# First three projection units multiplied with the unnormed x, with their sums scaled afterwards

## The chip, the cores and the metric

The kernel runs on one core of a Trainium2 chip. The metric is the device time in microseconds of one execution; of several runs the median is taken. TensorE (PE) multiplies, VectorE (DVE), ScalarE (ACT) and GpSimd (POOL) do the elementwise work, and SyncE (SP) issues the transfers.

## The reference

Three transformer-like layers over one sequence of 512 frames with 1024 channels, in float32. Only the first steps of the first layer matter here: a root-mean-square norm of x with a weight per channel, and a projection of the normed rows, whose columns are the q, k and v of eight heads and more.

```python
def rms_norm(x, w):
    xf = x.astype(jnp.float32)
    y = xf * lax.rsqrt(jnp.mean(xf * xf, axis=-1, keepdims=True) + EPS)
    return (y * w.astype(jnp.float32)).astype(x.dtype)

def hybrid_layer(x, pre_mix_norm, w_in, ...):
    h = rms_norm(x, pre_mix_norm)
    proj = h @ w_in
    q, k, v, z_a, b_a, a_a, z_s, x_s, b_s, c_s, dt_s = jnp.split(proj, offsets, axis=-1)
    qkv = jax.nn.silu(causal_dwconv(jnp.concatenate([q, k, v], axis=-1), gdn_conv_w))
    q = l2_normalize(q.reshape(bsz, s, GDN_HEADS, GDN_DK)) * (GDN_DK ** -0.5)
    ...
```

The factor rsqrt(mean(x*x)) belongs to a frame, the weight to a channel. All later layers (two more mixers and three feed-forward blocks) are the same in both kernels.

## The kernel before, in words

Channels lie on the 128 partitions and the 512 frames in the free dimension, so x is eight tiles X[k] of 128x512 (KD = 8). A weight unit is 128 output channels, loaded as raw (128x1024) by SP into one of four buffers. To keep float32 precision, each operand is split into a high part in fp32r and a low part, the rest: ACT copies (split_hi, L188), DVE subtracts (split_lo, L194), and PE takes three matmuls of 512 columns for each k: high by high, high by low, low by high. A unit is 24 matmuls. Units are counted from 1 here, as u0 + n in the code; unit n uses weight n - 1 (raw0, early[0] for unit 1).

The order on each engine is the program order, written out by hand, with semaphores between them. It begins with the stage "norm" and then "l1", the first layer's mixer:

- SP loads x in four transfers of two tiles, then the ones matrix and the norm's weights (params_in), then raw0 to raw3; later the other parameters, tab_w (the 32 columns of the tables) and, once POOL has cleared `small`, sixteen stores of zeros.
- norm_act squares X[k] (L339), splits weight 0, makes ln and exp(-0.5 ln) of the mean (rms_act, L266 and L268: the inverse root rs), and makes the high parts HH[k] of the normed tiles. norm_dve adds the squares (L302), makes normed_x[k] = X[k] * weight * rs (L308) and the low parts HL[k] (L312), with the low parts of weights 0 to 2 between them.
- norm_pe sums the squares over the partitions with one matmul by ones (L273). begin_pe then multiplies units 1 and 2 (q and k of head 0) in turns of k, as HL[k] comes; before the last k it puts the tables' eight float32 matmuls (L1461), which need all of normed_x. tables_pe (L1449) turns the tables once ACT has copied them (L1392).
- prep_pe goes on with unit 3 (q of head 1), the chunk sums (L1478), unit 4 (k of head 1), the ones-matmuls for q's and k's norms (L1758), the decays (L1768) and the products (L1730). From unit 5 on, a head takes some 15 us. ACT and DVE apply the four convolution taps to the sums in PSUM (tap_act L1493, tap_dve L1503), then silu, squares and norms.

Of the kernel before, what the change touches and what calls it, by code (L numbers as in the profile page):

```python
# [20 lines left out]
F32 = mybir.dt.float32  # L21
F32R = mybir.dt.float32r
# [42 lines left out]
def program(nc, x_in, w8, w11, par_in, cst_in, small_in, out, plan):  # L65
    cols = columns()
    ctx = ExitStack()
    with ctx:
# [42 lines left out]
        def tile(t, k):  # L111
            return t[:, k * S:(k + 1) * S]
# [42 lines left out]
        out_stored = sem("out_stored")  # L155

        NORM_COLUMNS, ALL_PARAMS = 9, 16 * 9
# [112 lines left out]
        def norm_pe(pe, c):  # L270
            pe.wait_ge(params_in, 32)
            pe.wait_ge(sq_added, c["add"] + KD - 1)
            nc.tensor.matmul(ss[:, :], ones, hn[0][:, :], start=True, stop=True).then_inc(sq_summed, 1)  # L273


# [3 lines left out]
        tab_w = place("tab_w", KD * NARROW, FREE + 17 * TILE)  # L279
        normed_x = place("normed_x", KD * S, FREE + 40 * TILE)  # L280

        fold = place("fold", NARROW, FREE + 16 * TILE)

        def norm_act(act, c, made):
            for k in range(KD):
                act.wait_ge(*made(k))
                square(act, c, tile(X, k), k, sq, hn[0])
            split_hi(act, 0, None, 0, KD, early[0])
            act.wait_ge(params_in, 32)
            rms_act(act, c["ssum"] + 1, c["rms"], D)  # L290
            split_hi(act, 1, None, 0, KD, early[1])
            for k in range(KD):
                act.wait_ge(hn_ready, c["hn"] + k + 1)
                nc.scalar.activation(tile(HH, k), tile(normed_x, k), ACT.Copy).then_inc(hh_ready, 1)
            split_hi(act, 2, None, 0, KD, None, 2 * SPLIT)

        def norm_dve(dve, c, gain):
            for k in range(1, KD):
                dve.wait_ge(sq_ready, c["sq"] + k + 1)
                if k > 1:  # L300
                    dve.wait_ge(sq_added, c["add"] + k - 1)
                nc.vector.tensor_tensor(hn[0][:, :], hn[0][:, :], sq[k % 2][:, :], ALU.add).then_inc(sq_added, 1)  # L302
            split_lo(dve, 0, None, 0, KD, early[0])
            dve.wait_ge(params_in, 32)
            dve.wait_ge(rms_ready, c["rms"] + 1)
            for k in range(KD + 1):
                if k < KD:
                    nc.vector.scalar_tensor_tensor(out=tile(normed_x, k), in0=tile(X, k), scalar=col(gain[0], gain[1] + k),  # L308
                                                   in1=rs[:, :], op0=ALU.mult, op1=ALU.mult).then_inc(hn_ready, 1)
                if k:  # L310
                    dve.wait_ge(hh_ready, c["hh"] + k)
                    nc.vector.tensor_tensor(tile(HL, k - 1), tile(normed_x, k - 1), tile(HH, k - 1).bitcast(F32),  # L312
                                            ALU.subtract).then_inc(h_ready, 1)
                if k == 1:
                    split_lo(dve, 1, None, 0, KD, early[1])
            split_lo(dve, 2, None, 0, KD)
# [1135 lines left out]
        def begin_pe(pe, c):  # L1452


            for k in range(KD):
                pe.wait_ge(h_ready, c["h"] - KD + k + 1)
                if k == KD - 1:
                    pe.wait_ge(params_in, ALL_PARAMS)
                    for j in range(KD):
                        g = j % 4  # L1460
                        last = nc.tensor.matmul(bank[5][NARROW * g:NARROW * (g + 1), :], tab_w[:, NARROW * j:NARROW * (j + 1)],  # L1461
                                                tile(normed_x, j), start=j < 4, stop=j >= 4, skip_group_check=True)
                    last.then_inc(a_pe, 1)
                for m in range(2):
                    a, (wh, wl) = bank[3 + m], (x[:, k * P:(k + 1) * P] for x in early[m])
                    if k == 0:
                        pe.wait_ge(w_lo_ready, m + 1)
                    nc.tensor.matmul(a[:, :], wh, tile(HH, k), start=k == 0, stop=False)
                    nc.tensor.matmul(a[:, :], wh, tile(HL, k), start=False, stop=False)
                    last = nc.tensor.matmul(a[:, :], wl, tile(HH, k), start=False, stop=k == KD - 1)  # L1470
                    if k == KD - 1:
                        last.then_inc(unit_done, 1)
# [101 lines left out]
        g_zero, c_inv = sem("l_zero_ready"), sem("l_inverse_step")  # L1574
# [9 lines left out]
        def prep_act(act, c):  # L1584
# [12 lines left out]
            act.wait_ge(unit_done, u0 + 2)  # L1597
# [4 lines left out]
            for h in range(1, NH + 1):  # L1602
                p = h - 1
                act.wait_ge(unit_done, u0 + 2 * h + 1)
                if p >= 2:
                    act.wait_ge(c_n, 2 * p - 2)
                tap_act(act, c, k_conv(p))
# [13 lines left out]
                if h >= 2:  # L1621
                    act.wait_ge(c_n, 2 * h - 2)
                tap_act(act, c, q_conv(h) if h < NH else v_conv(0))
# [65 lines left out]
        def prep_dve(dve, c):  # L1689
# [3 lines left out]
            for b in (1, 2, 3):  # L1693
                tap_dve(dve, c, q_conv(0), b)
            softplus_dve(dve)
# [26 lines left out]
        def prep_pool(pool, c):  # L1722
            nc.gpsimd.memset(l_inv[:, :], 0.0).then_inc(g_zero, 1)
# [18 lines left out]
        def prep_pe(pe, c):  # L1742
            def unit(n, part=None):

                multiply(pe, c["u"] + n, n % 2 if n in (3, 4) else c["t"] + n, None, 0, 0, KD, HH, HL, part=part)
# [3 lines left out]
            for h in range(1, NH + 1):  # L1749
                p = h - 1  # L1750
                unit(1 + 2 * h)
                if p == 0:
                    chunk_sums_pe(pe)
                    unit(2 + 2 * h)
                    pe.wait_ge(a_steps, 8)
# [387 lines left out]
        def load_l1(sp, c):  # L2143
# [39 lines left out]
            for n, k in enumerate(place_of, 1):  # L2183
                u = c["u"] + n
                if u >= RAW:
                    sp.wait_ge(w_lo_ready, u - RAW + 1)
                sp.dma_start(raw[u % RAW][:, 0:KD * P], w8[c["w8"] + k:c["w8"] + k + 1, :, :].rearrange(
                    "a p c -> p (a c)")).then_inc(raw_in[u % RAW], 16)
                if n == 4:
                    sp.wait_ge(params_in, 32)  # L2190
# [491 lines left out]
        made = lambda k: (x_loaded[k // 2], 16)  # L2682
# [3 lines left out]
        for at_, (kind, arg) in enumerate(plan):  # L2686
# [7 lines left out]
            if kind == "norm":  # L2694
                stages.append((kind, arg, c, made))
                for key, more in (("sq", KD), ("ssum", 1), ("add", KD - 1), ("rms", 1), ("hn", KD), ("hh", KD), ("h", KD)):
                    n[key] += more
# [26 lines left out]
            elif kind == "l1":  # L2724
                stages.append((kind, arg, c, None))
                for key, more in (("u", 53), ("t", 53), ("w8", 53), ("hh", 2 * KD), ("h", 2 * KD)):
                    n[key] += more
# [23 lines left out]
        def _(sp):  # L2751
            for k in range(0, KD, 2):
                sp.dma_start(X[:, k * S:(k + 2) * S], x_in[:, k * S:(k + 2) * S]).then_inc(x_loaded[k // 2], 16)
            sp.dma_start(cst[:, 0:2 * P], cst_in[:, 0:2 * P]).then_inc(params_in, 16)
            sp.dma_start(par[:, 0:NORM_COLUMNS], par_in[:, 0:NORM_COLUMNS]).then_inc(params_in, 16)
# [49 lines left out]
        def _(dve):  # L2805
            for kind, arg, c, more in stages:
                if kind == "norm":
                    norm_dve(dve, c, arg)
# [22 lines left out]
        def _(pool):  # L2831
            for kind, arg, c, more in stages:
                if kind == "later":
# [147 lines left out]
```

## Time and profile before

| | us |
|---|---|
| median of 3 runs | 2153.03 |
| lowest and highest run | 2147.13, 2154.74 |
| the profiled execution | 2149.57 |
| its span | 2147.8 |
| PE busy in the span | 2098.5 (98%) |
| DVE, ACT, POOL busy | 1212.0, 906.0, 326.6 |

A row of the timeline gives start, duration, engine, line, operation, output<-inputs, shapes, count, and in brackets the idle time before it with what ended it. The granted clock in the profile is a share of 2.4 GHz. For the first 23 us its column shows 1.00, but the matmuls' pitch there is 0.43 us, that of the stretches with 0.50, and changes to 0.23 at about 23.1: up to then the level was the lower one, 1.2 GHz.

### The profile page before, as it was taken

What the parts mean: (1) busy time and instruction counts of PE and PEld (TensorE: products, weight loads), DVE (VectorE), ACT (ScalarE), POOL (GpSimd) and SP (SyncE); (2) the same over time, 40 slices, a digit from 0 to 9 for tenths busy, and PEclk for the clock granted to TensorE, in tenths of its full rate; (3) what the DMA queues carried; (4) which work ended last, traced back from release to release, by engine and by line L of the source; (5) the groups of instructions that cost most, each with busy time, mean ns of one, the idle gap of its engine ahead of it and who ended that gap; (6) DMA issues with size and microseconds to landing.
All of it is one profiled execution on the core that took longest, in us unless ns stands there. A gap on an engine that the chain in (4) does not pass through costs nothing.

```text
span 2147.8 us, 26841 instructions
## 1 busy us (share of the span) xinstructions
PE 2098.5 (98%) x9776; PEld 1699.6 (79%) x9776; DVE 1212.0 (56%) x1663; ACT 906.0 (42%) x1282; POOL 326.6 (15%) x266
## 2 busy tenths in 40 slices
PE   6999999999999999999999999999999999999999
PEld 4778888878868888887766888888868878888887
DVE  5898755765366666225544566653354465666522
ACT  5883445434244444224564444442242354444411
POOL 0001221220112222001301122220000012222200
PEclk9999999999999999999999999999999999999999
DMA  7323222122212223222211232332222122222321
GB/s 235 94 75 96 82 77 71 49 69 73 95 67 94 93 96 120 95 82 67 69 40 49 89 98 98 98 114 94 86 69 88 60 73 94 98 98 97 115 95 66
DMA packets 81481, 188.96 MB, mean 88 GB/s; under 512 B 19824, under 2 KB 40432, under 8 KB 81392
## 3 DMA queue, kind: packets, MB, share of 16 engines
q1 hardware_dynamic: 81392, 187.75, 26.9%
q8 instruction: 59, 0.97, 0.2%
q14 instruction: 30, 0.25, 0.0%
HBM read 178.28 MB, written 9.44 MB: 87 GB/s over the span
## 4 chain that ended last, share of the span: by engine, by line
PE 92%; DVE 4%; ACT 2%; issue 1%; DMA 0%; POOL 0%; SPq 0%; DVEq 0%; ACTq 0%
PE acc L256 23%; PE acc L258 23%; PE acc L257 23%; PE bank L1248 1%; PE bank L232 1%; PE bank L1730 1%; PE bank L234 1%; PE bank L233 1%; PE acc L2636 1%; PE acc L2637 1%; PE acc L2638 1%; PE bank L2021 1%; PE bank L256 1%; PE bank L258 1%; PE bank L257 1%
## 5 line engine op out<-in xcount | busy, mean ns | idle before, releaser
L256 PE MATMUL acc<-HH,whi 128*128 128x512 f32 x1600 | 644.1, 403 | 6.8 <-DVE wlo L194 4.3
L258 PE MATMUL acc<-HH,wlo 128*128 128x512 f32 x1600 | 626.2, 391 | 0.0
L257 PE MATMUL acc<-HL,whi 128*128 128x512 f32 x1600 | 625.3, 391 | 0.0
L188 ACT ACTIVATE whi<-raw 128x1024 fp32r<-128x1024 f32 (+1 forms) x293 | 324.1, 1107 | 567.0 <-PE acc L258 537.7
L194 DVE TENSOR_TENSOR wlo<-raw,whi 128x1024 fp32r<-128x1024 f32 (+1 forms) x293 | 399.7, 1365 | 283.3 <-ACT whi L188 283.3
L256 PEld LDWEIGHTS acc<-HH,whi 128*128 128x128 f32 x1600 | 302.1, 189 | 73.8 <-DVE wlo L194 9.5
L258 PEld LDWEIGHTS acc<-HH,wlo 128*128 128x128 f32 x1600 | 301.5, 188 | 64.8
L257 PEld LDWEIGHTS acc<-HL,whi 128*128 128x128 f32 x1600 | 302.3, 189 | 62.5 <-issue 4.1
L256 PE MATMUL acc<-FH,whi 128*128 128x512 f32 x528 | 205.8, 390 | 0.0
L257 PE MATMUL acc<-FL,whi 128*128 128x512 f32 x528 | 205.4, 389 | 0.0
L258 PE MATMUL acc<-FH,wlo 128*128 128x512 f32 x528 | 205.4, 389 | 0.0
L391 DVE TENSOR_TENSOR acc<-acc,rs 128x512 f32<-128x512 f32 x150 | 104.8, 699 | 176.7 <-PE acc L258 176.7
L483 POOL TENSOR_TENSOR taps<-taps,taps 128x512 f32<-128x512 f32 x66 | 85.5, 1296 | 508.5 <-DVE taps L469 453.5
L448 ACT ACTIVATE FH<-taps 128x512 f32 (+1 forms) x66 | 41.7, 633 | 199.4 <-POOL taps L483 199.4
L256 PEld LDWEIGHTS acc<-FH,whi 128*128 128x128 f32 x528 | 99.1, 188 | 20.9 <-issue 0.2
L257 PEld LDWEIGHTS acc<-FL,whi 128*128 128x128 f32 x528 | 99.1, 188 | 20.9 <-issue 0.2
L258 PEld LDWEIGHTS acc<-FH,wlo 128*128 128x128 f32 x528 | 99.1, 188 | 20.5
L346 POOL TENSOR_TENSOR hn<-hn,sq 128x512 f32<-128x512 f32 x24 | 36.8, 1531 | 412.4 <-ACT sq L339 412.4
L469 DVE SCALAR_TENSOR_TENSOR taps<-acc,par,taps 128x510 f32<-128x510 f32 x117 | 87.6, 748 | 14.7 <-DVE taps L465 0.5
L488 POOL TENSOR_TENSOR FL<-taps,FH 128x512 f32 (+1 forms) x66 | 85.5, 1295 | 59.9 <-ACT FH L448 59.9
L439 ACT ACTIVATE taps<-acc,par 128x512 f32<-128x512 f32 x117 | 89.1, 762 | 0.6 <-DVE acc L391 0.6
L465 DVE SCALAR_TENSOR_TENSOR taps<-acc,par,taps 128x511 f32<-128x511 f32 x117 | 86.7, 741 | 0.0
(393 smaller groups left out, 2666.8 us busy)
## 6 DMA issues: line engine op xcount, KB each, us to landing
raw<-w SPq DMA_DIRECT2D x257, 512.0 KB, 3.5
raw<-w SPq DMA_DIRECT2D x48, 704.0 KB, 3.9
X<-x SPq DMA_DIRECT2D x4, 512.0 KB, 5.4
x_dram<-small SPq DMA_DIRECT2D x8, 256.0 KB, 4.3
xt_dram<-small SPq DMA_DIRECT2D x8, 256.0 KB, 3.7
a_dram<-l_am SPq DMA_DIRECT2D x8, 256.0 KB, 3.4
l_xt<-xt_dram SPq DMA_DIRECT2D x8, 256.0 KB, 3.3
l_x<-x_dram SPq DMA_DIRECT2D x8, 256.0 KB, 3.2
```

The lines of the kernel that those rows point to most:

```text
L188: nc.scalar.activation(hi[:, 0:kt * P], raw[u % RAW][:, 0:kt * P], ACT.Copy).then_inc(w_hi_ready, 1)
L194: nc.vector.tensor_tensor(lo[:, 0:kt * P], raw[u % RAW][:, 0:kt * P], hi[:, 0:kt * P].bitcast(F32), ALU.subtract).then_inc(w_lo_ready, 1)
L256: nc.tensor.matmul(a[:, :], wh, tile(hi, k), start=start and k == 0, stop=False)
L257: nc.tensor.matmul(a[:, :], wh, tile(lo, k), start=False, stop=False)
L258: last = nc.tensor.matmul(a[:, :], wl, tile(hi, k), start=False, stop=stop and k == kt - 1)
L391: nc.vector.tensor_tensor(a[:, :], a[:, :], rs[:, :], ALU.mult).then_inc(scaled, 1)
L439: nc.scalar.activation(taps[j][:, :], a[:, :], ACT.Identity, scale=w(2), bias=w(3)).then_inc(tap_ready, 1)
L448: nc.scalar.activation(o, taps[j - 1][:, :], ACT.Copy).then_inc(fh_ready, 1)
L465: nc.vector.scalar_tensor_tensor(out=taps[j][:, 1:S], in0=a[:, 0:S - 1], scalar=w(1), in1=taps[j][:, 1:S], op0=ALU.mult, op1=ALU.add).then ...
L469: nc.vector.scalar_tensor_tensor(out=taps[j][:, 2:S], in0=a[:, 0:S - 2], scalar=w(0), in1=taps[j][:, 2:S], op0=ALU.mult, op1=ALU.add).then ...
L483: nc.gpsimd.tensor_tensor(taps[2 * b][:, :], taps[2 * b][:, :], taps[2 * b + 1][:, :], ALU.mult).then_inc(prod_ready, 1)
L488: nc.gpsimd.tensor_tensor(o, taps[2 * b][:, :], h.bitcast(F32), ALU.subtract).then_inc(f_ready, 1)
```

## The change

Multiplying by the frame's factor can be done after the projection, since it doesn't depend on the channel. The change makes XH and XL, the high and low parts of X[k] * weight, without the factor, and multiplies units 1, 2 and 3 with them (m in the diff). DVE then multiplies the three sums in PSUM by rs (raw_scaled) before their taps. normed_x, HH and HL are still made, for the tables and for all later units; HL is now made by POOL. The squares are shared: ACT takes tiles 0, 2, 4, 6, DVE tiles 1, 3, 5, 7; POOL adds the first six, and PE adds three matmuls by ones. Four matmuls of zeros stand ahead of PE's first unit. Unit 3 is done in two halves, round the tables' matmuls. SP issues the nine columns of par first, then x0/1, raw0, the rest of x, the ones, raw1 and so on. Unit 4 has the chunk sums between its third and fourth part.

```diff
         def norm_act(act, c, made):
             for k in range(KD):
                 act.wait_ge(*made(k))
-                square(act, c, tile(X, k), k, sq, hn[0])
-            split_hi(act, 0, None, 0, KD, early[0])
-            act.wait_ge(params_in, 32)
-            rms_act(act, c["ssum"] + 1, c["rms"], D)
+                nc.scalar.activation(tile(XH, k), tile(X, k), ACT.Copy, scale=col("g_pre_mix", k)).then_inc(hh_ready, 1)
+                if k == 1:
+                    split_hi(act, 0, None, 0, KD, early[0])
+                if k % 2:
+                    nc.scalar.activation(first_sq[k - 1][:, :], tile(X, k - 1), ACT.Square).then_inc(sq_ready, 1)
             split_hi(act, 1, None, 0, KD, early[1])
+            rms_act(act, 3, c["rms"], D)
+            split_hi(act, 2, None, 0, KD, None, 2 * SPLIT)
             for k in range(KD):
                 act.wait_ge(hn_ready, c["hn"] + k + 1)
                 nc.scalar.activation(tile(HH, k), tile(normed_x, k), ACT.Copy).then_inc(hh_ready, 1)
-            split_hi(act, 2, None, 0, KD, None, 2 * SPLIT)
-        def norm_dve(dve, c, gain):
...
+        def norm_dve(dve, c, gain, made):
+            for k in range(KD):
+                dve.wait_ge(hh_ready, c["hh"] + k + 1)
+                nc.vector.scalar_tensor_tensor(out=tile(XL, k), in0=tile(X, k), scalar=col(gain[0], gain[1] + k),
+                                               in1=tile(XH, k).bitcast(F32), op0=ALU.mult,
+                                               op1=ALU.subtract).then_inc(h_ready, 1)
+                if k == 1:
+                    split_lo(dve, 0, None, 0, KD, early[0])
+                if k % 2:
+                    dve.wait_ge(*made(k))
+                    nc.vector.tensor_tensor(first_sq[k][:, :], tile(X, k), tile(X, k), ALU.mult).then_inc(dve_squared, 1)
+            split_lo(dve, 1, None, 0, KD, early[1])
+            dve.wait_ge(rms_ready, c["rms"] + 1)
+            for k in range(KD):
+                nc.vector.scalar_tensor_tensor(out=tile(normed_x, k), in0=tile(X, k), scalar=col(gain[0], gain[1] + k),
+                                               in1=rs[:, :], op0=ALU.mult, op1=ALU.mult).then_inc(hn_ready, 1)
+                if k == 1:
+                    split_lo(dve, 2, None, 0, KD)
+                if k == 3:
+                    raw_scaled(dve, 1)
+            raw_scaled(dve, 2)
+        def raw_scaled(dve, m):
+            dve.wait_ge(unit_done, m)
+            a = raw_acc({"t": 0}, m)
+            nc.vector.tensor_tensor(a[:, :], a[:, :], rs[:, :], ALU.mult).then_inc(scaled, 1)
+        def norm_pool(pool, c):
+            nc.gpsimd.memset(small[:, :], 0.0).then_inc(g_zero, 1)
+            for k in range(1, ADDED + 1):
...
+                nc.gpsimd.tensor_tensor(first_sq[0][:, :], first_sq[0][:, :], first_sq[k][:, :], ALU.add).then_inc(sq_added, 1)
+            for k in range(KD):
+                pool.wait_ge(hh_ready, c["hh"] + KD + k + 1)
+                nc.gpsimd.tensor_tensor(tile(HL, k), tile(normed_x, k), tile(HH, k).bitcast(F32),
+                                        ALU.subtract).then_inc(h_ready, 1)
+        def norm_pe(pe, c):
+            pe.wait_ge(g_zero, 1)
+            for _ in range(4):
+                nc.tensor.matmul(bank[1][:, :], small[:, 0:P], small[:, 0:S], start=True, stop=True)
+            pe.wait_ge(w_lo_ready, 1)
+            raw_unit(pe, c, 1)
+            pe.wait_ge(params_in, 16)
+            square_done(pe, ADDED + 1)
+            nc.tensor.matmul(ss[:, :], ones, first_sq[ADDED + 1][:, :], start=True, stop=False).then_inc(sq_summed, 1)
...
+            nc.tensor.matmul(ss[:, :], ones, first_sq[0][:, :], start=False, stop=True).then_inc(sq_summed, 1)
+            pe.wait_ge(w_lo_ready, 2)
+            raw_unit(pe, c, 2)
+            pe.wait_ge(w_lo_ready, 3)
+            raw_unit(pe, c, 3, 0, KD // 2)
         def begin_pe(pe, c):
...
+            pe.wait_ge(params_in, ALL_PARAMS)
+            pe.wait_ge(hn_ready, KD)
+            for j in range(KD):
+                g = j % 4
+                last = nc.tensor.matmul(bank[5][NARROW * g:NARROW * (g + 1), :], tab_w[:, NARROW * j:NARROW * (j + 1)],
+                                        tile(normed_x, j), start=j < 4, stop=j >= 4, skip_group_check=True)
+            last.then_inc(a_pe, 1)
+            raw_unit(pe, c, 3, KD // 2)
         def prep_dve(dve, c):
...
                 tap_dve(dve, c, q_conv(0), b)
+            raw_scaled(dve, 3)
             softplus_dve(dve)
             for n, k in enumerate(place_of, 1):
                 u = c["u"] + n
+                if n == 2:
+                    for m in range(1, KD // 2):
+                        sp.dma_start(X[:, 2 * m * S:2 * (m + 1) * S], x_in[:, 2 * m * S:2 * (m + 1) * S]).then_inc(x_loaded[m], 16)
+                    sp.dma_start(cst[:, 0:2 * P], cst_in[:, 0:2 * P]).then_inc(params_in, 16)
```

raw_unit is the loop of 24 matmuls (three for each k) over XH and XL into the unit's PSUM bank; for m = 1 it waits for XL[k] at each k. ADDED is 5. ACT's taps of the three units now wait for `scaled`.

## Rows read from the trace of the kernel before

**Rows 1.** page, part 4: the chain that ended last, by engine.
```profile
PE 92%; DVE 4%; ACT 2%; issue 1%; DMA 0%; POOL 0%; SPq 0%; DVEq 0%; ACTq 0%
```

**Rows 2.** timeline, 4 to 12 us: start, duration, engine, line, operation, count, [idle before].
```profile
4.87 2.07 ACT L339 ACTIVATE sq<-X 128x512 f32<-128x512 f32 x3
...
8.10 1.15 ACT L339 ACTIVATE sq<-X 128x512 f32<-128x512 f32 x2 [1.16 <-DMA X<-x]
...
10.07 1.15 ACT L339 ACTIVATE sq<-X 128x512 f32<-128x512 f32 x2 [0.82 <-DMA X<-x]
...
11.79 1.06 ACT L188 ACTIVATE early_hi<-raw 128x1024 fp32r<-128x1024 f32 x1 [0.56 <-DMA raw<-w]
```

**Rows 3.** timeline, 12 to 17 us; last, one line's own view: min/median/max ns.
```profile
12.37 2.04 PE L273 MATMUL bank<-hn,cst 128*128 128x512 f32 x2 [12.37 <-DVE hn L302]
...
15.96 1.42 DVE L308 SCALAR_TENSOR_TENSOR normed_x<-X,par,rs 128x512 f32<-128x512 f32 x2 [1.86 <-DMA par<-par]
...
L323 ACT ACTIVATE HH<-X,par x16: 722/724/727, 597.7 to 990.6; 128x512 fp32r<-128x512 f32 x16
```

**Rows 4.** one piece of the chain (start, length); then PE's timeline, 24 to 35 us.
```profile
22.37 0.43 PE bank L1468
...
24.71 0.39 PE L1468 MATMUL bank<-HH,early_hi 128*128 128x512 f32 x1
...
29.92 0.39 PE L1470 MATMUL bank<-HH,early_lo 128*128 128x512 f32 x1
...
30.24 1.92 PE L1461 MATMUL bank<-normed_x,tab_w 128*32 128x512 f32 x16
...
33.60 0.97 PE L1449 MATMUL bank<-fold,l_tab 128*128 128x32 f32 x8
```

**Rows 5.** timeline, 34 to 53 us, engines DVE, ACT and PE.
```profile
34.97 1.21 DVE L194 TENSOR_TENSOR wlo<-raw,whi 128x1024 fp32r<-128x1024 f32 x1
...
40.82 0.41 ACT L1411 ACTIVATE t_exp<-bank 128x288 f32<-128x288 f32 x1 [1.28 <-PE bank L1478]
...
46.12 1.88 PE L1758 MATMUL bank<-l_sq,cst 128*128 128x512 f32 x4
...
50.16 1.16 PE L1730 MATMUL bank<-l_kn 128*128 128x128 f32 x8 [1.27 <-DVE l_kn L1712]
...
52.32 0.47 PE L256 MATMUL acc<-HH,whi 128*128 128x512 f32 x1
```

**Rows 6.** timeline, POOL and DVE, where both run: 614 and 1753 to 1783 us.
```profile
614.09 4.91 POOL L374 TENSOR_TENSOR squares<-squares 128x512 f32<-128x512 f32 x3 [30.85 <-ACT squares L324]
...
614.99 1.50 DVE L194 TENSOR_TENSOR wlo<-raw,whi 128x1024 fp32r<-128x1024 f32 x1 [0.71 <-ACT whi L188]
...
1753.48 1.86 POOL L346 TENSOR_TENSOR hn<-hn,sq 128x512 f32<-128x512 f32 x1 [184.45 <-ACT sq L339]
...
1753.45 0.74 DVE L364 SCALAR_TENSOR_TENSOR HL<-X,par,HH 128x512 fp32r<-128x512 f32 x1
...
1781.55 1.38 POOL L346 TENSOR_TENSOR hn<-hn,sq 128x512 f32<-128x512 f32 x1 [4.44 <-ACT sq L339]
...
1781.70 1.78 DVE L364 SCALAR_TENSOR_TENSOR HL<-X,par,HH 128x512 fp32r<-128x512 f32 x1
```

**Rows 7.** timeline, POOL and DVE at 636 us, DVE with an operand in PSUM.
```profile
636.55 1.28 POOL L483 TENSOR_TENSOR taps<-taps,taps 128x512 f32<-128x512 f32 x1 [4.20 <-DVE taps L469]
...
636.32 0.69 DVE L391 TENSOR_TENSOR bank<-bank,rs 128x512 f32<-128x512 f32 x1
```

**Rows 8.** stretches: length, busy time of each engine, granted clock; then PE's timeline.
```profile
170.00:176.70 6.70, 5.02 (x38) 4.47 (x36) 4.83 (x13) 1.17 (x3) 1.82 (x2) 1.00 0.62 174
176.80:183.50 6.70, 6.19 (x22) 5.42 (x23) 3.82 (x11) 1.82 (x3) 0.65 (x1) 0.50 0.33 87
...
1743.50:1746.80 3.30, 3.30 (x10) 2.52 (x9) 1.85 (x3) 2.19 (x3) 0.00 (x0) 0.50 0.47 159
...
1743.09 0.50 PE L256 MATMUL acc<-PH,whi 128*128 128x512 f32 x1 [2.86 <-DVE PL L767]
```

More of the change, by code:

```diff
@@ new lines, in raw_unit @@
+        def raw_unit(pe, c, m, k0=0, k1=KD):
+            a, (wh, wl) = raw_acc(c, m), early[m - 1] if m < 3 else (whi[0], wlo[0])
+            for k in range(k0, k1):
+                if m == 1:
+                    pe.wait_ge(h_ready, c["h"] + k + 1)
+                h, l = (w[:, k * P:(k + 1) * P] for w in (wh, wl))
+                nc.tensor.matmul(a[:, :], h, tile(XH, k), start=k == 0, stop=False)
+                nc.tensor.matmul(a[:, :], h, tile(XL, k), start=False, stop=False)
+                last = nc.tensor.matmul(a[:, :], l, tile(XH, k), start=False, stop=k == KD - 1)
+            if k1 == KD:
+                last.then_inc(unit_done, 1)
@@ L1606, in prep_act @@
                     act.wait_ge(c_n, 2 * p - 2)
+                elif p == 0:
+                    act.wait_ge(scaled, 2)
                 tap_act(act, c, k_conv(p))
@@ L1743, in unit @@
             def unit(n, part=None):
-                multiply(pe, c["u"] + n, n % 2 if n in (3, 4) else c["t"] + n, None, 0, 0, KD, HH, HL, part=part)
+                multiply(pe, c["u"] + n, n % 2 if n == 4 else c["t"] + n, None, 0, 0, KD, HH, HL, part=part,
+                         ready=(h_ready, c["h"] - KD) if n == 4 else None)
             begin_pe(pe, c)
@@ L1750, in prep_pe @@
                 p = h - 1
[L1751 to L1754, printed above, removed]
+                if p:
+                    unit(1 + 2 * h)
+                else:
+                    for part in range(4):
+                        unit(4, part)
+                        if part == 2:
+                            chunk_sums_pe(pe)
                     pe.wait_ge(a_steps, 8)
@@ L2695, in program @@
                 stages.append((kind, arg, c, made))
-                for key, more in (("sq", KD), ("ssum", 1), ("add", KD - 1), ("rms", 1), ("hn", KD), ("hh", KD), ("h", KD)):
+                for key, more in (("sq", KD - len(BY_DVE)), ("ssum", 3), ("add", ADDED), ("rms", 1), ("hn", KD), ("hh", 2 * KD), ("h", 2 * KD)):
                     n[key] += more
@@ L2725, in program @@
                 stages.append((kind, arg, c, None))
-                for key, more in (("u", 53), ("t", 53), ("w8", 53), ("hh", 2 * KD), ("h", 2 * KD)):
+                for key, more in (("u", 53), ("t", 53), ("w8", 53), ("hh", 2 * KD), ("h", 2 * KD), ("scaled", 3)):
                     n[key] += more
@@ L2751, in _ @@
         def _(sp):
[L2752 to L2755, printed above, removed]
+            sp.dma_start(par[:, 0:NORM_COLUMNS], par_in[:, 0:NORM_COLUMNS]).then_inc(x_loaded[0], 16)
+            sp.dma_start(X[:, 0:2 * S], x_in[:, 0:2 * S]).then_inc(x_loaded[0], 16)
             if plan[1][0] != "l1":
@@ L2832, in _ @@
             for kind, arg, c, more in stages:
-                if kind == "later":
+                if kind == "norm":
+                    norm_pool(pool, c)
+                elif kind == "later":
                     squares_pool(pool, c, sq, hn[0])
```

83 lines of the change are left out of this document (33 added, 50 removed).

## The prediction

> **What bounds the kernel now.** I read the page's chain of waits first: TensorE (PE) holds 92% of it [rows 1], so only work that PE waits for can move the end, and only where PE now has gaps. The timeline then shows where these are. PE does nothing of weight before 12.37 (one ones-matmul for the norm), starts the projection at 18.16 and is then unbroken to about 50, where it waits 1.27 us for k's norm; from 52.32, the first matmul of unit 5, it runs dense again [rows 4, 5]. The reader is to see that the change touches only what lies ahead of 52.32, and that the question is when that matmul starts. Ahead of it lie three serial stretches: x arrives and is squared and added (to 12.4), the inverse root is made and handed on (15.96) [rows 2, 3], and after the tables' matmuls of L1449 at 33.60 a chain over VectorE (DVE) and ScalarE (ACT) to 52.32, 18.7 us long [rows 4, 5].
>
> **What the change gives PE.** Units 1 and 2 and half of 3 (60 matmuls, 0.227 us each at the high clock: 23 from 24.71 to 29.92 in [rows 4], so 13.6 us) no longer wait for the root. At most this frees the time from about 8.5, when the first weights are split, to 18.16: some 10 us. It can be kept only if the root and all that hangs on it come no later, since L1461 (tables) still needs all eight normed_x. So the sum is the time of the eighth normed_x.
>
> **Arrival.** par's nine columns go first, one issue more, for which I take 0.45 us; raw0 goes third instead of seventh. The transfers land in their slots: by [rows 2] the first at 4.34, the second by about 5.6 (the squares run on from 4.87), the third 8.10, the fourth 10.07, raw0 at 11.79. Shifted: x0/1 at 4.8, raw0 at 6.1 (estimate, 5.6 to 7), then x2/3 8.5, x4/5 10.4, x6/7 12.1. DVE's speed, not these, sets what follows. The tables' weights and the rest of par are issued near where they were and are needed only after 26 us; the sixteen zero stores stay off the chain.
>
> **ACT and DVE up to the root, taken alone.** ACT's scaled copy is 0.72 us [rows 3], its split 1.05: hi of raw0 at 7.2. DVE: the low part is a three-operand instruction of 0.75 (0.67 from start to start; L308's and L364's form), a square 0.69 (0.61), a weight's low part 1.22 (1.13) [rows 3, 5, 6]. Weight 0 is ready at 8.45; then one square, six low parts and three squares, 6.5 us, with a short wait for ACT: last low part 14.5, last square 15.1. PE ends unit 1 at 15.2 and adds three ones-matmuls, 0.86 each (L1758: four halves, 1.88) [rows 5], plus 0.2 of tail: 18.0. From the sum to DVE's first normed_x takes 1.55 (14.41 to 15.96) [rows 3]: 19.4 against 15.96 now. Then eight normed_x (5.4), one weight (1.13), one scaling (0.6): the eighth is done at 26.6. PE has ended its half unit by 26.2.
>
> **The path behind it.** Tables 1.85, the other half of unit 3 with its gap 2.95, so L1449 starts 4.9 us behind the eighth normed_x: 31.5 instead of 33.60. The chain after it costs 0.3 more than now: the weight's low part that used to run beside unit 3 is now waited for (2.6 us, L1449's start to 36.18), then 18 matmuls (4.1) and the chunk sums follow. Now it is L1449 0.97, 24 matmuls 5.45, the sums the other 0.8 of the 7.2 to 40.82 [rows 4, 5]; then 2.6 + 4.1 + 0.8 = 7.5; the extra scaling of 0.7 hides beside these matmuls. Taken alone, the change would give 2.1 - 0.3 = **1.8 us**, not ten: the rest comes back as PE's waits. The four zero matmuls are nothing on the path: 4 x 1.7 us from 1.7 to at most 8.6, just under the weight's 8.45.
>
> **The term that turns it: POOL beside DVE.** The change moves five adds and eight low parts to GpSimd (POOL) while DVE is busy without a break. [rows 6] are what these two do to each other when both read two operands from SBUF. POOL asked at 1753.48, DVE was 0.03 us into an instruction of 0.74, and POOL's add took 1.86 instead of 1.29; at 1781.55 POOL was first, and DVE's low part took 1.78 instead of 0.75. At 614 both had more to do, and they took turns: three adds in 4.91 (3.9 alone) round a split of 1.50. [rows 7] is the control: a DVE instruction with an operand in PSUM ran beside POOL at full speed. In the change DVE's low parts, squares, splits and normed_x all have two SBUF operands; only the scalings have not. So each turn of POOL while DVE has work costs DVE 1.29 less overlaps of 0.15 and 0.2, near 1.0 us (a pair takes 1.7, DVE alone 0.67). The bounds are 0 (as [rows 7]) and 1.29, a whole add; I take 1.0, the rows of this very form.
> Up to the root: add 1 starts at 9.15, right ahead of low part 2; each later add waits for its square and gets the next turn. DVE then reads low part 2 until 11.0, 3 until 12.7, square 3 13.35, 4 14.0, 5 15.75, square 5 17.4, 6 18.1, 7 19.8, square 7 20.4; add 5 ends at 19.2. Five turns, 5.3 us. PE's unit 1 ends at 20.55, the sum at 23.25, DVE's first normed_x starts at **24.8**.
> After the root: POOL's low part k can start when ACT's high part k is there, one step behind normed_x k, so low parts 0 to 5 each take a turn ahead of normed_x 2 to 7: six turns, of which 0.5 us lies beside the scaling. 7.2 + 5.7 = 12.9, the eighth normed_x at **37.7**. POOL's last low part, 40.2, is in time for unit 4.
> L1449 then starts at 42.6 instead of 33.60: +9.0, with the chain's 0.3 **+9.3 us**.
>
> The Trainium skill, "SBUF — State Buffer", section "Who interferes with whom", speaks against this change in the same words: a VectorE instruction with two SBUF inputs contends with a GpSimd instruction that reads SBUF, one blocks for the whole of the other. By it eleven turns would cost 11 x 1.29 = 14.2 us less what lies beside the scaling; the rows, with their overlaps at both ends, say 11. The trace agrees with it [rows 6, 7].
>
> **The clock.** In the new unit 1, PE works 0.7 us in each 1.7 us turn (40%), and before the tables it stands idle from 31.4 to 37.7. [rows 8] show what follows that: after a stretch with 5.0 busy of 6.7 us, and after one wait of 2.86 us, the granted clock was 0.50 (1.2 GHz; its pitch is the 0.43 of the piece at 22.37 [rows 4]) for 6.8 and 3.3 us. At that level the three ones-matmuls and unit 1's last step cost up to 3.1 us more on the path (I take 2.4: it should come back during them), the tables and the half unit 1.6 + 2.4 = 4.0 more (I take 3.0). Bounds for both together: 0 and 7.1.
> The Trainium skill, "TensorE: Matmul & The Clock Gate", section "HAM oscillation — how this bites in real kernels", has the rule that waits between bursts of matmuls send the engine back to half clock. It would make the sum the higher one; [rows 8] agree.
>
> **Sum.** 9.3 + 2.4 + 3.0 = 14.7, taken as +14 because the turns' ends are rough. The profiled execution, 2149.57 (span 2147.8), would become 2163.6; the median of the runs is 3.5 above it, so **2167** against 2153.03. About 0.5% (10.8 us) is what a measurement of this kernel can tell from no change; the chances below use it.
>
> **Rivals.**
> 1. Turns and clock as above, +10 to +19: 2163 to 2172. Chance 0.48.
> 2. Turns, but the clock stays high (against it [rows 8]; for it, that PE was never idle for long in unit 1): +9.3, 2162. Chance 0.20.
> 3. No turns, the other side: DVE and POOL run beside each other, as in [rows 7]. The deciding point is the first normed_x: while it starts before about 21.2 (4.9 and 0.3 and 7.2 us ahead of 33.60), the change isn't slower. Price -1.8: 2151. Against it is every overlap in [rows 6]; for it only that no row shows a square x*x or normed_x beside POOL. Chance 0.12.
> 4. Turns that cost half, because x comes later and DVE has holes in which POOL's work fits: +3 to +8, 2158. Chance 0.08.
> 5. The clock falls a further time under unit 4 or the squares' ones-matmuls, whose chain has little room: +20 to +25, 2175. Chance 0.10.
> 6. Something takes the chain after L1449 along, and all ten us are kept: 2143. Chance 0.02.
>
> **Range.** Without the lowest case and part of 3 and 5: 2152 to 2176. Slower by over 0.5%: most of 1 (0.42), all of 5 (0.10), the upper edge of 2 (0.04), 0.56. Faster by over 0.5%: 0.02. Within: 0.42.
>
> **What would show it.** In the changed kernel's timeline: the low parts of x at 1.7 to 1.8 us instead of 0.75 and POOL's adds at up to 1.9; the first normed_x near 25 to 27 (right) or near 19 (rival 3); normed_x records of 1.8 next to POOL's low parts; PE idle for some 5 us ahead of the tables; a granted clock of 0.50 in one or two stretches before 50; unit 5 starting near 66 instead of 52.32, and the rest of the trace merely shifted. Wrong would be: normed_x at 0.75 throughout, weight 0 ready far from 8.5, or a later stage that gives the shift back.

## The result and the profile after

The median went from 2154.0 us to **2166.1 us** (five runs each, 2147.1 to 2154.7 and 2165.2 to 2166.2); the ratio is 1.0069, with an interval of 1.0056 to 1.0082. The prediction was 2167, slower by over 0.5%. The profiled execution took 2165.16, its span 2163.4 against 2147.8. The page of after has the same shape, and its chain is PE for 91% [rows 1]:

```profile
PE 2112.3 (98%) x9788; PEld 1705.8 (79%) x9788; DVE 1223.3 (57%) x1663; ACT 908.1 (42%) x1286; POOL 347.0 (16%) x279
...
PE 91%; DVE 5%; ACT 3%; issue 1%; DMA 0%; POOL 0%; SPq 0%; ACTq 0%; DVEq 0%
```

Nothing there tells where 12 us went. The beginning of the timeline does. Of the kernel after, DVE and POOL from 6 to 41 us (start, duration, engine, line, operation, count, idle time before it):

```profile
6.14 1.42 DVE L313 SCALAR_TENSOR_TENSOR XL<-X,par,XH 128x512 fp32r<-128x512 f32 x2 [6.14 <-ACT XH L298]
...
9.50 2.45 DVE L313 SCALAR_TENSOR_TENSOR XL<-X,par,XH 128x512 fp32r<-128x512 f32 x2
11.87 1.77 DVE L320 TENSOR_TENSOR first_sq<-X 128x512 f32<-128x512 f32 x1
...
17.63 2.42 DVE L313 SCALAR_TENSOR_TENSOR XL<-X,par,XH 128x512 fp32r<-128x512 f32 x2
19.97 0.68 DVE L320 TENSOR_TENSOR sq<-X 128x512 f32<-128x512 f32 x1
...
25.97 1.42 DVE L324 SCALAR_TENSOR_TENSOR normed_x<-X,par,rs 128x512 f32<-128x512 f32 x2 [4.18 <-ACT rs L269]
...
28.43 3.48 DVE L324 SCALAR_TENSOR_TENSOR normed_x<-X,par,rs 128x512 f32<-128x512 f32 x2
31.84 0.68 DVE L336 TENSOR_TENSOR bank<-bank,rs 128x512 f32<-128x512 f32 x1
32.44 6.19 DVE L324 SCALAR_TENSOR_TENSOR normed_x<-X,par,rs 128x512 f32<-128x512 f32 x4
...
9.73 3.36 POOL L346 TENSOR_TENSOR first_sq<-first_sq,first_sq 128x512 f32<-128x512 f32 x2 [8.04 <-DVE first_sq L320]
...
27.48 13.51 POOL L349 TENSOR_TENSOR HL<-normed_x,HH 128x512 fp32r<-128x512 f32 x8 [7.98 <-ACT HH L308]
```

A pair of low parts takes 1.42 before POOL starts and 2.45 beside its adds; a square takes 1.77 in place of 0.68 (the last one, alone again, 0.68); two normed_x take 3.48 in place of 1.42. POOL's eight low parts fill 13.51, 1.69 each. Nowhere is DVE shown as waiting for POOL (the 4.18 us ahead of 25.97 are for the root): the turns are inside the durations. The scaling at 31.84, whose second operand lies in PSUM, kept its 0.68 beside POOL, as [rows 7] had it.

PE of the kernel after, up to unit 5:

```profile
1.75 5.30 PE L368 MATMUL bank<-small 128*128 128x512 f32 x8 [1.75 <-POOL small L339]
9.04 0.50 PE L359 MATMUL bank<-XH,early_hi 128*128 128x512 f32 x1 [1.99 <-DVE early_lo L195]
...
21.55 1.28 PE L373 MATMUL bank<-sq,cst 128*128 128x512 f32 x2
...
38.77 3.64 PE L1523 MATMUL bank<-normed_x,tab_w 128*32 128x512 f32 x16 [6.06 <-DVE normed_x L324]
...
45.27 0.97 PE L1514 MATMUL bank<-fold,l_tab 128*128 128x32 f32 x8
...
63.73 1.16 PE L1788 MATMUL bank<-l_kn 128*128 128x128 f32 x8 [1.25 <-DVE l_kn L1771]
...
65.88 0.48 PE L257 MATMUL acc<-HH,whi 128*128 128x512 f32 x1
```

PE starts its first unit 9 us earlier than before (18.16 there), and then stands still for 6.06 us ahead of the tables, because the eighth normed_x ends only at 38.63. The tables' turning (L1514) starts at 45.27 instead of 33.60, unit 5 at 65.88 instead of 52.32 [rows 4, 5]: 13.6 us late. Four stretches of after: length, busy time of PE, its weight loads, DVE, ACT and POOL, then the granted clock (0.50 in all four), DMA share and GB/s:

```profile
18.70:22.00 3.30, 3.09 (x7) 1.85 (x7) 3.08 (x3) 0.00 (x0) 0.80 (x1) 0.50 0.28 99
35.80:42.50 6.70, 3.73 (x17) 0.84 (x17) 3.44 (x3) 1.40 (x3) 5.29 (x5) 0.50 0.64 194
49.40:52.70 3.30, 3.30 (x9) 2.57 (x8) 2.56 (x6) 0.90 (x2) 0.00 (x0) 0.50 0.36 129
59.70:63.00 3.30, 2.78 (x10) 1.95 (x8) 3.07 (x5) 3.24 (x5) 0.00 (x0) 0.50 0.00 0
```

It fell to 0.50 four times before unit 5: from 18.7 to 22.1 (sparse unit 1), from 35.7 to 42.5 (it fell during the idle time), and twice in the chain behind the tables. Before had none of these once its clock had risen at 23.1.

### The profile page after: what moved, and what is told of

It is laid out like the page before. It is cut to its first block, busy times and chain, and to the rows that moved or that the text cites. A ratio compares the mean times of both kernels' runs of the same rounds, so it can differ in the third digit from the quotient of the medians.

```text
span 2163.4 us, 26878 instructions
## 1 busy us (share of the span) xinstructions
PE 2112.3 (98%) x9788; PEld 1705.8 (79%) x9788; DVE 1223.3 (57%) x1663; ACT 908.1 (42%) x1286; POOL 347.0 (16%) x279
## 4 chain that ended last, share of the span: by engine, by line
PE 91%; DVE 5%; ACT 3%; issue 1%; DMA 0%; POOL 0%; SPq 0%; ACTq 0%; DVEq 0%
PE acc L257 23%; PE acc L259 23%; PE acc L258 23%; PE bank L1313 1%; PE bank L1788 1%; PE bank L233 1%; PE bank L235 1%; PE bank L234 1%; PE acc L2705 1%; PE acc L2703 1%; PE acc L2704 1%; PE bank L2083 1%; PE bank L257 1%; PE bank L259 1%; PE bank L258 1%
## 5 line engine op out<-in xcount | busy, mean ns | idle before, releaser
L257 PEld LDWEIGHTS acc<-HH,whi 128*128 128x128 f32 x1592 | 300.6, 189 | 75.4 <-DVE wlo L195 12.1
```

The costliest lines, as they stand in the source:

```text
L257: nc.tensor.matmul(a[:, :], wh, tile(hi, k), start=start and k == 0, stop=False)
```

## The experiments

Start times are from the profiled executions, ratios from all runs of a kernel against the runs of before on the same chip (whose median moved between 2148.5 and 2154.0 from batch to batch, so that ratios and positions are compared, not medians). The theory is the prediction's: turns of 1 us between POOL and DVE in two places, and the clock. "Late" is the time from the first normed_x to the end of the eighth; in after it is 12.66.

**POOL's low parts moved behind the eighth normed_x.**

```diff
+            pool.wait_ge(hn_ready, c["hn"] + KD)
             for k in range(KD):
                 pool.wait_ge(hh_ready, c["hh"] + KD + k + 1)
```

> The kernel after, but POOL starts its eight low parts HL only when the eighth normed_x is done (one wait more on POOL, nothing else). Theory (POOL and DVE take turns when both read two operands from SBUF, about 1.0 us lost to DVE for each turn): normed_x records of 0.75 again, the eighth done 7.2 to 7.3 us after the first starts (33.2 instead of 38.6), PE idle under 1 us before the tables, so their clock stays at 1.00, L1514 at 38, unit 5 near 57 instead of 65.9, time 2157 (2155 to 2159). Rival (the loss comes from the later root alone, the spread of normed_x is DVE's own pace or its waits for ACT): the eighth normed_x stays near 38.6 and the time near 2166, or higher since HL comes later.

Ratio 1.004 (1.0026 to 1.0054), 2159.7 us. DVE and POOL of this kernel:

```profile
26.81 1.42 DVE L324 SCALAR_TENSOR_TENSOR normed_x<-X,par,rs 128x512 f32<-128x512 f32 x2 [4.72 <-ACT rs L269]
...
31.21 2.73 DVE L324 SCALAR_TENSOR_TENSOR normed_x<-X,par,rs 128x512 f32<-128x512 f32 x4
...
34.02 11.00 POOL L350 TENSOR_TENSOR HL<-normed_x,HH 128x512 fp32r<-128x512 f32 x8 [14.21 <-DVE normed_x L324]
```

From first to eighth took 7.13 us instead of 12.66: the six turns behind the root cost **5.5 us**. Nothing else on DVE differs in that stretch, and the adds' turns ahead of it stayed as they were. The time was a little above the expected range, and unit 5 came at 57.8 where 57 was expected: a low clock from 16.6 to 23.5 held the root up (first normed_x at 26.81 instead of 25.97), and what was lost behind unit 5 is in the table of the next section.

**The five adds left out**, and **both at once**. Here PE sums one square in place of the six added ones (part of the norm's sum is missing).

```diff
-            for k in range(1, ADDED + 1):
...
-                nc.gpsimd.tensor_tensor(first_sq[0][:, :], first_sq[0][:, :], first_sq[k][:, :], ALU.add).then_inc(sq_added, 1)
...
-            pe.wait_ge(sq_added, c["add"] + ADDED)
+            square_done(pe, 0)
```

> The kernel after without POOL's five adds of squares: the mean holds only three of the eight squares, so this leaves out five additions. Theory of turns: DVE's low parts of x and squares fall back to 0.75 and 0.69, the last square ends at about 15.6 instead of 20.6, the first normed_x starts at 20.1 instead of 26.0; behind the root the turns stay, PE is idle some 6 us before the tables and their clock is 0.50 again; unit 5 near 60, time 2160 (2158 to 2162). Rival (the root is late because x and the weights arrive late, or because PE adds three ones-matmuls): the first normed_x stays within 1 us of 26.0 and the time at 2166.

> Both: no adds on POOL (five of eight squares left out of the mean) and POOL's low parts only after the eighth normed_x, so POOL never reads SBUF beside DVE in this stretch. Theory: the sum of the forecast without turns, started 0.6 us later as weight 0 was: first normed_x 20.1, eighth done 27.4, L1514 32.3 against 33.60 in the kernel before, unit 5 at 51.3 against 52.32: 2151 to 2154, no difference from the kernel before that can be told. The two gains add: 5.9 + 8.8 us. Rival (multiplying the raw x frees ten us of PE and something else ate them): clearly faster than before, 2145 or less, or still over 2160 if the turns weren't the cause.

Without the adds: ratio 1.0044 (1.0027 to 1.0061), 2160.5 us. Without both: **1.0007** (0.9998 to 1.0017), 2152.4 us. DVE, then PE, of the kernel without both:

```profile
11.29 1.41 DVE L313 SCALAR_TENSOR_TENSOR XL<-X,par,XH 128x512 fp32r<-128x512 f32 x2
12.61 0.68 DVE L320 TENSOR_TENSOR first_sq<-X 128x512 f32<-128x512 f32 x1
...
19.67 1.42 DVE L324 SCALAR_TENSOR_TENSOR normed_x<-X,par,rs 128x512 f32<-128x512 f32 x2 [3.32 <-ACT rs L269]
...
24.07 2.73 DVE L324 SCALAR_TENSOR_TENSOR normed_x<-X,par,rs 128x512 f32<-128x512 f32 x4
...
26.94 1.92 PE L1517 MATMUL bank<-normed_x,tab_w 128*32 128x512 f32 x16 [0.48 <-DVE normed_x L324]
31.65 0.97 PE L1508 MATMUL bank<-fold,l_tab 128*128 128x32 f32 x8
```

The first normed_x moved from 25.97 to 19.67, 6.3 us, in both kernels; the turning of the tables came at 31.65, 1.95 us ahead of before. That is the change "taken alone". It shows two things: all the slowness ahead of the tables is POOL's two blocks beside DVE (with the clock that they bring down), and the change without them is still worth only 2 us. The additions left out were not on the path themselves: in after POOL's last one ends at 19.50 (17.78 and 1.72), ahead of DVE's last square, which ends at 20.65 and at 15.22 without them. So what they cost is what they add to DVE's durations, 5.4 us.

**The factor read from PSUM.** Same work and same order on DVE and POOL, POOL beside normed_x; only the place of one operand is another, and ACT has one instruction more. ACT writes rs to a free PSUM bank first, then to SBUF.

```diff
+            nc.scalar.activation(bank[2][:, :], ln[:, :], ACT.Exp, scale=-0.5).then_inc(rs_in_psum, 1)
+            nc.scalar.activation(rs[:, :], ln[:, :], ACT.Exp, scale=-0.5).then_inc(rms_ready, 1)
...
-                                               in1=rs[:, :], op0=ALU.mult, op1=ALU.mult).then_inc(hn_ready, 1)
+                                               in1=bank[2][:, :], op0=ALU.mult, op1=ALU.mult).then_inc(hn_ready, 1)
```

> The kernel after, but ACT writes the inverse root a second time, into a free PSUM bank, and normed_x reads it there: the same work in the same order on DVE and POOL, one ACT instruction of 0.63 more, only the place of one operand is another. Theory: DVE then reads one operand from SBUF, so there are no turns beside POOL but the one at the split of weight 2: normed_x records 0.75, POOL's adds and low parts 1.29, the eighth normed_x done near 34, L1514 near 39, time 2158 (2156 to 2160). Rival (the two engines delay each other through semaphores or order, not through the SBUF reads): normed_x records stay near 1.75 and the time near 2166.

```profile
31.22 2.71 DVE L329 SCALAR_TENSOR_TENSOR normed_x<-X,par,bank 128x512 f32<-128x512 f32 x4
...
28.73 10.55 POOL L355 TENSOR_TENSOR HL<-normed_x,HH 128x512 fp32r<-128x512 f32 x8 [9.00 <-ACT HH L313]
```

Ratio 1.0025 (1.001 to 1.004), 2158.1 us. Four normed_x take 2.71 in the middle of POOL's block, and POOL's low parts 1.32 each instead of 1.69. So the cause, for normed_x, is the second SBUF operand and not the company of POOL as such. For the low parts of x and the squares no run moved an operand to PSUM; there the same cause is taken from the same added time. The Trainium skill, "SBUF — State Buffer", section "Who interferes with whom", says that a VectorE instruction with at most one SBUF input, outside the engine's two-port modes, doesn't contend with GpSimd; this run agrees (2.71 us for four).

**The clock.** Idle matmuls keep PE busy in the two sparse places: four after each of the steps 3 to 6 of unit 1, 24 ahead of the tables.

```diff
+                if m == 1 and 3 <= k <= 6:
+                    filler(4)
...
             raw_unit(pe, c, 3, 0, KD // 2)
+            filler(24)
```

> The kernel after with idle matmuls in PE's waits: four of 0.23 us after each of the steps k = 3 to 6 of unit 1, and 24 (5.5 us) after the first half of unit 3, where PE waits 6.06 us for the eighth normed_x. Their sums are never read. Theory (the granted clock falls because PE waits, and the fall costs): no stretch at 0.50 at 18.65 and 35.7 any more; the first normed_x starts 1.0 to 1.5 us earlier than 25.97, the tables take 1.9 instead of 3.64, L1514 starts 3 us earlier than 45.27: 2163 (2161.5 to 2165). Rival (the clock costs nothing, since PE is off the chain there): time and L1514 unchanged within 0.5 us, or later, because the idle matmuls stand in the way.

Ratio 1.0066 (1.0048 to 1.0083). PE and, last, a stretch, of this kernel:

```profile
20.97 1.02 PE L379 MATMUL bank<-sq,cst 128*128 128x512 f32 x2
...
38.02 1.92 PE L1530 MATMUL bank<-normed_x,tab_w 128*32 128x512 f32 x16 [0.68 <-DVE normed_x L324]
42.74 0.97 PE L1521 MATMUL bank<-fold,l_tab 128*128 128x32 f32 x8
```

The clock stayed high from 7.9 to 45.5 us. From the end of the last XL to the first normed_x is 5.0 us here (20.13 to 25.13) and 5.9 in after (20.05 to 25.97); from the tables to their turning 4.7 (38.02 to 42.74) and 6.5 in after. So the low clock cost after 0.9 and 1.8 us ahead of the turning, not 2.4 and 3.0. The first normed_x came 0.84 us earlier and the turning 2.5, both a little less than expected. Two low stretches still fell in the chain behind, at 45.5 and 55.7, and at unit 5 2.2 us of the gain were left. The total hardly moved (1.0066 against 1.0069): the trace ends 15.1 us late instead of 15.6, with 3.4 us more of low clock behind unit 5.

**Without the four zero matmuls.**

```diff
-            for _ in range(4):
-                nc.tensor.matmul(bank[1][:, :], small[:, 0:P], small[:, 0:S], start=True, stop=True)
```

> The kernel after without the four zero matmuls ahead of unit 1. Theory: PE starts at 9.0 at the lower level; unit 1's steps take 1.28 us instead of 0.7, still within the 1.7 to 2.0 us that DVE's turns take, so only the two first steps and the ones-matmuls can be late. First normed_x between 0.3 earlier and 2.5 later than 25.97, time 2167 (2165 to 2169). Rival (the warm start carries the ones-matmuls' clock and is worth several us): 2170 or more.

Ratio 1.0064 (1.0046 to 1.0082), no other than after's 1.0069 within these intervals. The median, 2161.7, is below the expected range, but before's median was 2149.6 beside it and 2154.0 beside after. What failed is the bound on the first normed_x, "0.3 earlier" at most. Unit 1 began at 9.02 at the low level, but the clock rose at 12.5 and then stayed up to 36.4, so the first normed_x came at 24.97, a microsecond before that of after. The zero matmuls bought nothing: PE's unit 1 waits for DVE at either level.

**The loads in their old order** (x and the ones ahead of the weights; par stays first).

```diff
-                if n == 2:
-                    for m in range(1, KD // 2):
...
+            for m in range(KD // 2):
+                sp.dma_start(X[:, 2 * m * S:2 * (m + 1) * S], x_in[:, 2 * m * S:2 * (m + 1) * S]).then_inc(x_loaded[m], 16)
```

> The kernel after with x and the ones loaded ahead of all weights, as in the kernel before; only par's nine columns stay first. Theory: raw0 lands near 11.8, ACT's split of it then ends at 12.9 instead of 7.7, and since it stands ahead of ACT's copies of x2 and later, DVE's turns start 5 us later: first normed_x near 31, time 2171 (2169 to 2173). So the new order of loads is worth 5 us inside the change. Rival (DVE and POOL, not the loads, set the root, and the order of loads is worth nothing): first normed_x within 1 us of 25.97, time 2166.

Ratio 1.0098 (1.0078 to 1.0118), 2169.0 us, the slowest of all. Weight 0's low part starts at 12.08, after 5.00 us of waiting for its high part, the last XL ends 4.3 us later than in after, the first normed_x comes at 31.66 (the low clock costs 2.3 here), unit 5 is 18.6 us late instead of 13.6. The early weight is worth 5 us to this change, in line with DVE being what sets the pace.

**A version meant to be without the turns, with all of the work.** Squares are rounded to fp32r and summed by eight one-pass matmuls between the last steps of unit 1 (no adds); POOL's low parts wait for the eighth normed_x; weight 3's low part and the first taps go ahead of the tables' steps on DVE and ACT; the chunk sums stand after the second part of unit 4.

```diff
-            nc.tensor.matmul(ss[:, :], ones, first_sq[ADDED + 1][:, :], start=True, stop=False).then_inc(sq_summed, 1)
...
+            return nc.tensor.matmul(ss[:, :], ones_r[:, :], first_sq[j][:, :], start=j == 0, stop=j == KD - 1)
...
+            pool.wait_ge(hn_ready, c["hn"] + KD)
...
-            tables_dve(dve)
             split_lo(dve, u0 + 4, None, 0, KD)
...
             raw_scaled(dve, 3)
+            tables_dve(dve)
...
-                        if part == 2:
+                        if part == 1:
                             chunk_sums_pe(pe)
```

> What the change's idea gives when DVE and POOL don't meet and the chain behind the root is shortened: squares rounded to fp32r and summed by eight one-pass matmuls in and behind unit 1 (no adds on POOL, no float32 ones-matmuls), POOL's low parts behind the eighth normed_x, weight 3's low part and the first taps ahead of the tables on DVE and ACT, chunk sums after the second part of unit 4. Expected from the rows: last square 15.2, first normed_x 17.7, eighth done 25.0, tables' L1449 counterpart at 30, chunk sums at 34, unit 5 at 46.1 instead of 52.32 before: 2147 (2145 to 2150), faster than before by 0.2 to 0.4%. If the turns weren't the bound, or PE's own work is, it comes out at 2151 or more.

Ratio 1.0009 (0.9999 to 1.002), median 2151.3; 2147 was expected, and unit 5 came at 49.17 instead of 46.1. DVE, then PE:

```profile
18.55 1.41 DVE L327 SCALAR_TENSOR_TENSOR normed_x<-X,par,rs 128x512 f32<-128x512 f32 x2 [1.99 <-ACT rs L269]
...
34.19 1.45 DVE L1499 SCALAR_TENSOR_TENSOR t_soft<-l_arg,l_soft 128x128 f32<-128x128 f32 x1 [1.06 <-ACT l_soft L1471]
35.67 1.20 DVE L1502 SCALAR_TENSOR_TENSOR t_ld<-t_soft,raw 128x96 f32<-128x96 f32 x1
...
31.65 1.08 PE L1519 MATMUL bank<-fold,l_tab 128*128 128x32 f32 x8 [0.92 <-DVE l_q L1562]
36.93 0.91 PE L1537 MATMUL bank<-t_ld,cst 128*128 128x96 f32 x6 [1.39 <-DVE t_ld L1502]
```

Moved late, POOL's low parts meet two small DVE steps of the chain, which take 1.45 and 1.20 instead of 0.28 and 0.26, and PE waits 1.39 us for them. Some of the turns had been moved, not taken out.

**The same with POOL early and rs in PSUM**, and the turning waiting for l_tab alone (lines against the version above).

```diff
-            pool.wait_ge(hn_ready, c["hn"] + KD)
...
+                                               in1=bank[2][:, :], op0=ALU.mult, op1=ALU.mult).then_inc(hn_ready, 1)
...
-            pe.wait_ge(acc_read, c["t"] + 2)
+            pe.wait_ge(ones_ready, 2)
```

> The version of e8_reordered with its two remaining waits taken out: POOL makes HL beside the eight normed_x again, which now read the factor from PSUM as in e4_rs_psum, and the tables' turning matmuls wait for l_tab alone instead of l_tab and the taps. Theory (turns): normed_x stay at 1.4 a pair, the eighth near 25.7; POOL's low parts run from 20 to 30.5, so t_soft and t_ld, which took 1.45 and 1.20 in e8_reordered, take 0.3 each; tables' turning matmuls near 30.8 (31.65), chunk sums near 34.5 (36.93), products near 44.8 (47.02; before 50.16), some 5 us ahead of before. With the low-clock stretches landing anywhere, 2146 us (2142 to 2150), ratio 0.996 to 1.000. Rival (POOL beside DVE costs the same wherever it runs, in SBUF or PSUM): normed_x 1.8 each, the eighth near 30, 2152 or more.

```profile
33.90 0.29 DVE L1504 SCALAR_TENSOR_TENSOR t_soft<-l_arg,l_soft 128x128 f32<-128x128 f32 x1 [1.06 <-ACT l_soft L1476]
...
30.68 0.97 PE L1524 MATMUL bank<-fold,l_tab 128*128 128x32 f32 x8
34.54 0.91 PE L1544 MATMUL bank<-t_ld,cst 128*128 128x96 f32 x6
...
44.63 1.16 PE L1801 MATMUL bank<-l_kn 128*128 128x128 f32 x8 [2.58 <-DVE l_kn L1784]
```

Every step came where it was expected, the products 5.5 us ahead of before [rows 5], and yet the ratio is 0.9998 (0.9986 to 1.0009): the change, freed of its turns, is 0.7% faster than it was and not measurably faster than before; 2148.8 us and this ratio lie at the slow edge of what was expected. Where the 5.5 us went, the next section shows.

## What the clock does with a gain or a loss at the beginning

For each kernel: how much later than in before the same matmul starts, near unit 5 (60 us in the trace of before) and at the end, and for how long the records of the granted clock show 0.50 behind that point, leaving out a stretch that begins in the last 1.2 us (before: 20.5 us, in four stretches from 177 us on).

```
kernel                    near unit 5   at the end   low clock behind it
after                       +13.5         +15.6         23.9
POOL late                    +5.4         +10.0         30.7
no adds                      +6.3          +9.6         27.3
neither                      -1.3          +2.4         27.3
factor in PSUM               +5.6          +6.5         20.5
filler                      +11.4         +15.1         27.3
no zero matmuls             +11.9          +6.4          3.4
old loads                   +18.6         +19.5         17.1
without turns, late          -3.2          -4.1         17.1
without turns, early         -4.0          +1.8         34.1
```

The code from unit 5 on is the same in all of them, and what is lost or gained there goes with the last column: 13.6 us more at the low level cost the last kernel 5.7 us, 17.1 less gave the one without zero matmuls 5.5 back. Where the difference is over 6 us, each microsecond of it goes with 0.3 to 0.55; smaller ones fit less well (the old loads lost 1.0 with 3.4 less), so another microsecond or so hangs on which work a stretch falls on. The stretches of that last kernel:

```profile
172.20:182.30 10.10, 8.90 (x35) 7.84 (x34) 4.48 (x11) 2.49 (x4) 1.26 (x1) 0.50 0.22 57
226.80:233.50 6.70, 5.58 (x19) 5.03 (x20) 3.07 (x3) 0.68 (x2) 2.51 (x2) 0.50 0.58 134
465.80:472.40 6.60, 6.60 (x26) 5.57 (x26) 1.38 (x2) 0.34 (x1) 0.79 (x2) 0.50 0.00 0
```

Before had low clock at 177, but none at 227 or 466. Of the last kernel's 5.5 us at the products, 1.5 were gone by 60 us, with a low stretch from 45.9 to 49.3, and 5.7 more went behind that. These are single profiled executions, and two of them, of the kernel without zero matmuls (2155.96) and of the one without turns, late (2145.51), are the fastest runs of their kernels, so that their rows look better than their ratios. Which of the later thin places of PE get a low stretch varies from kernel to kernel, and a ratio from many runs holds the mean of it. Within the runs of one kernel it shows as the spread: 2142.5 to 2151.4 for the last one, 2143.7 to 2154.1 for before beside it.

The mean granted clock of every run says the same with more runs behind it. In the 16 runs of before beside the last kernel it goes from 0.998 to 0.992 as the time goes from 2143.7 to 2154.1; a straight line through them gives 0.39 us for each microsecond of low clock (an estimate, since the clock is known to 0.001 only; 0.33 and 0.41 in the two other batches of before). The last kernel's twelve runs have 0.9926 in the mean and before's 0.9950, which is about 10 us more of low clock (3.4 of them, in its trace, ahead of unit 5), worth some 4 us by that line. Compared at the same clock the last kernel is the faster one: its one run at 0.996 took 2142.5, before's four at 0.996 took 2147.2 to 2148.7. So the gain at the beginning was real, and in the mean of the runs, not only in one trace, more low clock stood against it. What decides where a stretch falls was not settled, and no run held the clock fixed, so this is a relation and not a shown cause.

## Why the prediction was right

Right in mechanism, and in number too, but that the number is so close is partly luck: one term was too large and two smaller ones were missing, and these cancelled.

- Arrival and first steps: weight 0 ready at 9.0 (8.45 forecast), last XL done at 20.05 (19.8), the zero matmuls off the path. Right.
- The change alone, -1.8 us (2.1 ahead at the tables' turning, 0.3 lost behind it): 1.95 ahead at the turning in the kernel without turns, 1.3 at unit 5, with a low stretch between the two. (18.0 and 1.55 are 19.55 in the recorded sum, not 19.4; the slip is of no weight.) Right, and with it the reading that DVE's serial work, not PE's, sets the eighth normed_x.
- Turns up to the root, 5.3 us: the first normed_x moved by 6.3, of which 0.9 is clock, so 5.4, as DVE's last square has it (20.65 and 15.22). Turns after it, 5.7 us: 5.5. Right; the price of 1.0 per turn from [rows 6] held for squares and normed_x, of which no row of before showed one.
- From the last XL to the first normed_x, 5.0 us at full clock: 5.0 in the filler kernel.
- The clock ahead of the tables' turning, 2.4 + 3.0: measured 0.9 + 1.8. This is the term that was mis-sized. One low stretch ended at 22.1, so that of the three ones-matmuls only the first had it, and the other at 42.5, right behind the tables, so that the half unit ran at the high level. The same term was 2.3 for the ones with the old loads and 1.4 with POOL late, so 2.4 was the upper end of what the runs show and not its middle.
- The chain behind the turning, +0.3: it was +1.9 (20.6 us from 45.27 to 65.88, before 18.7), since the clock fell twice in it; the filler kernel, also with two, paid 2.3, and the six kernels with one low stretch there 0.3 to 0.7. No kernel with this order of steps had none, so the 0.3 itself is not shown. The forecast had this as rival 5, on top of the rest, at 0.10: half of it came true, in place of the overestimated part.
- The rest of the trace "merely shifted": no, +2.0, with 3.4 us more of low clock than before.

The sum by the runs, in the profiled executions: -1.95 + 5.4 + 5.5 + 0.9 + 1.8 = 11.65 (33.60 to 45.27 is 11.67), + 1.9 + 2.0 = 15.6, against +14. By medians it is +12.1, because before's profiled execution was 4.4 us under that batch's median and after's 1.0: subtracting medians gives less than subtracting the traces.

Rivals 3 (no turns) and 6 (all ten us kept) are out by every kernel with the turns. Rival 4 (half the price) is out by the durations, 1.03 to 1.09 added per turn to low parts and squares. Rival 2 (turns, but a high clock) is what the filler kernel shows up to the turning, 9.1 late where 9.0 was forecast for that point; but the clock then fell in the chain behind, unit 5 was 11.4 late and the end 15.1. The Trainium skill, "TensorE: Matmul & The Clock Gate", section "HAM oscillation — how this bites in real kernels", lets waits between bursts bring the clock down; that agrees with the fall at 35.7, within the wait of 6.06 us, while what this cost the path was half of what was taken for it.

## What to carry to other kernels

Before work is moved to POOL, look at what DVE does beside it: here, when both read two SBUF operands, they take turns, and the cost (1 us for each 1.3 us instruction) is in DVE's durations and not in its waits; an operand in PSUM avoided it. Removing a dependency of PE frees only what the next chain leaves: here ten microseconds of early PE work were worth two, since the tables waited for the same eighth normed_x. And a few microseconds won or lost at the beginning of a long kernel are mixed with clock stretches hundreds of microseconds later, so judge such an edit by the shift of a fixed matmul right behind it, and the total by many runs.

## What the runs showed of the hardware that was not expected

- A square x*x, whose two inputs are one and the same SBUF tile, takes turns with POOL like any two-input instruction: 1.77 us beside an add, 0.68 alone.
- A small DVE instruction pays the same: 128x128 elements took 1.45 us beside POOL's low parts and 0.29 without them.
- Four zero matmuls that raised the clock at 5.0 us gave nothing: it fell at 18.7, while without them it rose at 12.5 and stayed up to 36.4.
- With equal code from unit 5 on and shifts of -4.0 to +18.6 us at its beginning, the low-clock time of the following 2.1 ms lay between 3.4 and 34.1 us, and with it the total moved by up to 5.7 us. The two kernels at -3.2 and -4.0 had 17.1 and 34.1.
